# Row loads and final stores on one queue: a Trainium2 encoder step with the loads of the next group placed further back

## What is computed

```
h = rmsnorm(x, norm1_g)
z = h @ w_in                       # 1024 -> 1536 = [a | u | v], 512 columns each
u, v = gelu(u), gelu(v)
pool_out = trailing means of a over 2, 4, 8, 16 rows, minus a, per-group 128x128 map, scale
gmlp_out = u * (W_s v + b)         # in chunks of 128 rows, 4 heads, block-causal mask
x = x + concat(pool_out, gmlp_out) @ w_out
f = rmsnorm(x, norm2_g) @ w_up     # 1024 -> 4096
x = x + square(relu(f)) @ w_down   # 4096 -> 1024
y = rmsnorm(x, normf_g)
```

## Time and profile before

| what | us |
|---|---|
| median of 3 runs | 1239.54 |
| lowest and highest of the 3 | 1237.45, 1247.37 |
| the profiled execution, whole | 1246.71 |
| its span on the slowest core (core 1) | 1245.2 |
| its span on the fastest core (core 7) | 1212.4 |
| PE busy on core 1 | 1179.2 (95%) |
| DVE, ACT, POOL busy on core 1 | 803.9, 438.2, 156.8 |

### The profile page before, as it was taken

One profiled execution on the slowest core, in us unless ns is written; L12 is line 12 of the kernel. 1 busy time (PEld: TensorE's weight loads), 2 busy tenths in 40 slices (PEclk: granted clock), 3 DMA queues, 4 the chain that ended last, 5 costly groups with the idle time before them and its releaser, 6 DMA issues.

```text
span 1245.2 us, 21470 instructions; the slowest of 8 cores (1212.4 to 1245.2 us)
## 1 busy us (share of the span) xinstructions
PE 1179.2 (95%) x7412; PEld 701.2 (56%) x7412; DVE 803.9 (65%) x1164; ACT 438.2 (35%) x678; POOL 156.8 (13%) x303
## 2 busy tenths in 40 slices
PE   6889999988999999999999999997999999999996
PEld 2547456533444577446754577445764576547842
DVE  3564545386567675867587675865778575976773
ACT  3446022323410454134530364132640365233401
POOL 3111000113000220022100220021100220011001
PEclk7999999999899989999999999998999999999998
DMA  9996798989995895769767794769856896869993
GB/s 197 167 212 168 210 249 208 209 327 311 331 310 196 261 311 176 255 228 314 270 228 235 263 332 165 267 217 305 281 199 224 252 371 135 299 201 324 307 330 130
DMA packets 64907, 310.41 MB, mean 249 GB/s; under 512 B 9872, under 2 KB 9936, under 8 KB 44064
## 3 DMA queue, kind: packets, MB, share of 16 engines
q1 hardware_dynamic: 48992, 239.35, 57.9%
q0 software_dynamic: 15664, 69.15, 21.8%
q10 hardware_dynamic: 144, 0.52, 0.2%
HBM read 277.90 MB, written 53.31 MB: 266 GB/s over the span
## 4 chain that ended last, share of the span: by engine, by line
PE 73%; DMA 17%; DVE 3%; issue 3%; ACT 2%; POOL 1%; DVEq 0%; POOLq 0%; SPq 0%; ACTq 0%
PE ps L757 23%; PE ps L668 20%; PE ps L538 9%; PE ps L419 9%; DMA scr_up<-RING 5%; DMA yall<-XS 5%; PE ps L440 4%; PE ps L619 3%; PE ps L594 3%; DMA RING<-w_mlp 2%; DMA RING<-scr_up 2%; PE ps L373 2%; DMA XS<-xall 1%; ACT JUNK L350 1%; DMA scr_um<-RING 1%
## 5 line engine op out<-in xcount | busy, mean ns | idle before, releaser
L757 PE MATMUL ps<-RING,ST 128*128 128x512 bf16 x1120 | 256.9, 379 | 0.3 <-DVE ST L730 0.3
L350 ACT ACTIVATE JUNK<-XS 128x1024 bf16<-128x1024 f32 (+1 forms) x100 | 105.5, 1055 | 315.3 <-DVE XS L543 228.9
L668 PE MATMUL ps<-H2T,RING 128*128 128x256 bf16 x1536 | 184.1, 278 | 16.6 <-DVE ST L709 15.0
L757 PEld LDWEIGHTS ps<-RING,ST 128*128 128x128 bf16 x1120 | 108.7, 98 | 126.5 <-issue 1.7
L668 PEld LDWEIGHTS ps<-H2T,RING 128*128 128x128 bf16 x1536 | 152.2, 100 | 47.8 <-issue 20.1
L767 DVE TENSOR_TENSOR XS<-XS,ps 128x512 f32<-128x512 f32 x140 | 95.8, 685 | 75.3 <-PE ps L757 70.8
L668 PE MATMUL ps<-SB,RING 128*128 128x256 bf16 x1152 | 138.8, 273 | 3.9 <-DMA RING<-scr_um 2.2
L668 PEld LDWEIGHTS ps<-SB,RING 128*128 128x128 bf16 x1152 | 111.3, 98 | 20.4 <-issue 5.6
L719 ACT ACTIVATE ST<-ST 128x1024 bf16<-128x1024 bf16 x96 | 101.4, 1056 | 54.9 <-DVE ST L709 50.5
L419 PE MATMUL ps<-HT,WAU 128*128 128x512 bf16 (+2 forms) x512 | 118.0, 379 | 1.4 <-ACT HT L377 1.4
L709 DVE TENSOR_TENSOR ST<-PQ,ps 128x512 bf16<-128x512 f32 x96 | 61.7, 684 | 64.7 <-ACT PQ L705 37.5
(11 more groups left out here) (107 smaller groups left out, 1421.6 us busy)
## 6 DMA issues: line engine op xcount, KB each, us to landing
RING<-scr_dn SPq DMA_DIRECT2D x98, 1024.0 KB, 6.3
RING<-scr_um SPq DMA_DIRECT2D x120, 512.0 KB, 7.8
RING<-scr_up SPq DMA_DIRECT2D x48, 512.0 KB, 8.9
RING<-w_mlp POOLq DMA_DIRECT2D x16, 1024.0 KB, 14.8
yall<-XS POOLq DMA_DIRECT2D x29, 512.0 KB, 8.4
RING<-scr_wo SPq DMA_DIRECT2D x14, 1024.0 KB, 5.8
XS<-xall POOLq DMA_DIRECT2D x24, 512.0 KB, 7.9
scr_up<-RING POOLq DMA_DIRECT2D x8, 1024.0 KB, 14.1
```

What stands on the lines that cost most here:

```text
L350: add("act", lambda e: e.activation(out=JUNK[0:np_], in_=ap, func=AF.Square, scale=1.0 / 32, accum_out=SS[kind][0:np_, j:j + 1]), reads=re ...
L668: i_ = e.matmul(bank(ub)[:, u * 256:(u + 1) * 256], lhsT=RING[s][:, h * 4 + k, c0 + u * 128:c0 + (u + 1) * 128], rhs=op[:, k, :], start=(f ...
L757: i_ = e.matmul(bank(ub)[:, :], lhsT=lh(kk), rhs=RING[s][:, kk, :], start=(c == 0 and kk == 0 and M not in CONT), stop=(c == 1 and kk == 7 ...
```

## The change

The steps of five kinds of side work are renumbered. No operation is added or taken away.

- The loads of tiles 1 and 2 of group i + 2 leave down steps 22 and 25 of group i. They are recorded with the load of tile 3 in the up stage of the group after: tiles 1, 2 and 3 at up steps 1, 3 and 7 (`lx=(1, 3, 7)`), where tile 3 alone stood at step 6. At steps 1 and 7 a `final_out` of the same step is recorded ahead of the load. The load of tile 0 stays at down step 3.
- The four gates of a down stage stand one step earlier (4, 4, 6, 6), except for those of the plain group.
- In the plain group `N1_sq` of tile 2 stands at step 21 instead of 19. The new entry `us` is not used, and `lx` there names the step that the loads had.
- In both setup passes the fourth weight sum stands at step 11 instead of 12 and the fifth at 16 instead of 14, each with its `ring_done`.
- In pass 1 the four transposes `N2_T` of group 2 stand one step earlier (4, 5, 7, 8).

```diff
-                ws = dict(w=(5, 6, 10, 12, 14))
+                ws = dict(w=(5, 6, 10, 11, 16))
...
-                    for n in range(4):
-                        side(8, L(load_x, j, n))
...
+                    for n in range(4):
+                        side(tn["lx"][n], L(load_x, j, n))
...
                     if j < NG:
-                        side(tn["lx"], L(load_x, j, 3))
+                        for n in range(3):
+                            side(tn["lx"][n], L(load_x, j, n + 1))
...
                     if i + 2 < NG:
-                        side(d(dn["lx"][0]), L(load_x, i + 2, 0))
+                        side(d(dn["lx"]), L(load_x, i + 2, 0))
                     for n in range(2):
                         side(d(dn["fq"][n]), L(final_sq, i, n), L(final_rs, n, n + 1))
                         side(d(dn["fo"][n]), L(final_out, i, n))
-                        if i + 2 < NG:
-                            side(d(dn["lx"][1 + n]), L(load_x, i + 2, n + 1))
```

More of the change, by code:

```diff
@@ L960, in schedule @@
                 else:
-                    e1 = dict(v=(1, 3), pl=(0, 1, 2, 3), gt=(8, 8, 9, 10), wo=(14, 15, 16, 17, 18, 19, 20, 21), nq=(21, 22, 23, 24), rs=(23, 23, 25, 25), na=(2, 3, 4, 5), nt=(5, 6, 8, 9), fq=(16, 17, 18), fo=(19, 19, 19))
+                    e1 = dict(v=(1, 3), pl=(0, 1, 2, 3), gt=(8, 8, 9, 10), wo=(14, 15, 16, 17, 18, 19, 20, 21), nq=(21, 22, 23, 24), rs=(23, 23, 25, 25), na=(2, 3, 4, 5), nt=(4, 5, 7, 8), fq=(16, 17, 18), fo=(19, 19, 19))
                     for n in range(2):
@@ L1005, in schedule @@
                 if plain:
+                    tn = dict(sq=(15, 17, 21, 21), ap=(18, 20, 22, 24), tr=(23, 27, 27, 30), v=(36, 37, 39, 39), au=(31, 31, 33, 34, 35, 36, 37, 38), pl=(34, 36, 38, 39), us=(7, 7, 7, 7), lx=(8, 8, 8, 8))
                     side(0, *[L(final_sq, 1, n) for n in range(2)], L(final_rs, 0, 2))
@@ L1008, in schedule @@
                     for n in range(4):
-                        side(8, L(load_x, j, n))
-                    tn = dict(sq=(15, 17, 19, 21), ap=(18, 20, 22, 24), tr=(23, 27, 27, 30), v=(36, 37, 39, 39), au=(31, 31, 33, 34, 35, 36, 37, 38), pl=(34, 36, 38, 39))
+                        side(tn["lx"][n], L(load_x, j, n))
                 else:
-                    tn = dict(sq=(2, 5, 7, 11), ap=(3, 6, 9, 12), tr=(5, 8, 11, 14), v=(6, 11, 14, 19), au=(15, 16, 18, 18, 20, 21, 23, 24), pl=(18, 18, 21, 22), fq=(0, 0), fo=(1, 7), lx=6)
+                    tn = dict(sq=(2, 5, 7, 11), ap=(3, 6, 9, 12), tr=(5, 8, 11, 14), v=(6, 11, 14, 19), au=(15, 16, 18, 18, 20, 21, 23, 24), pl=(18, 18, 21, 22), fq=(0, 0), fo=(1, 7), lx=(1, 3, 7))
                     for n in (2, 3):
@@ L1016, in schedule @@
                     if j < NG:
-                        side(tn["lx"], L(load_x, j, 3))
+                        for n in range(3):
+                            side(tn["lx"][n], L(load_x, j, n + 1))
                 d = lambda k: d0 + k
-                dn = dict(s1=(0, 1, 2, 3), s7=(5, 5, 8, 9), s2=(10, 10, 11, 11), s6=(11, 11, 13, 12), sm=(12, 12, 13, 13), fq=(18, 20), fo=(21, 24), lx=(3, 22, 25), gt=(5, 5, 7, 7), wo=(10, 11, 12, 13, 14, 15, 16, 17), nq=(14, 15, 16, 17), na=(16, 16, 17, 18), nt=(17, 18, 19, 21), es=(25, 25, 26, 27, 27), u1=25)
+                dn = dict(s1=(0, 1, 2, 3), s7=(5, 5, 8, 9), s2=(10, 10, 11, 11), s6=(11, 11, 13, 12), sm=(12, 12, 13, 13), fq=(18, 20), fo=(21, 24), lx=3, gt=(4, 4, 6, 6), wo=(10, 11, 12, 13, 14, 15, 16, 17), nq=(14, 15, 16, 17), na=(16, 16, 17, 18), nt=(17, 18, 19, 21), es=(25, 25, 26, 27, 27), u1=25)
                 if plain:
```

## The result

Over 20 runs each the changed kernel took 1249.6 us (median), the kernel before 1241.3 us. The ratio is 1.0074, with a 95% interval of [1.0055, 1.0093]; measured again later beside new runs of the kernel before it was 1.0043 [1.0024, 1.0062]. So the change costs some 0.4 to 0.7%: small, inside the 1% that the prediction named as its limit, and real. The ratios leave out executions in which cores of one die ran at a lower granted clock.

What follows compares the result with a forecast made beforehand. PE, busy 95% of the span, was taken as the bound. Core 3: 1229.5 + 9.5 (late rows) + 1.7 (setup) = 1240.7; core 1: 1223.7 + 9.5 + 1.7 = 1234.9; forecast 1238 us between them, range 1226 to 1254.

Steps and rivals of the forecast that it cites:

- The chain store, load, store, load, root is cut: POOL's queue: two store-load pairs, some 12 us each on core 1, no longer stand ahead of a root PE needs.
- Its worth: 22.0 us on core 1: PE's L709 waits, 15.0 us, plus 7.0 us of lowered clock are saved on core 1; 1.9 us on core 3.
- The profiled execution stands 7.2 us above the median: The profiled execution is 7.2 us above the median of the runs shown; the median should lie between cores 3 and 1.
- The weights' loads give back 3.0 us: Up stage, core 3: half of PE's 6.0 us of weight waits is regained, between 0 and 6.0; about 1 on core 1.
- The load of tile 1 comes 3.9 us late for ACT: Up stage, behind the store of tile 2: rows land at 571.1, 3.9 us after ACT wants them at 567.25.
- That costs PE 1.9 us a boundary, 9.5 in all: After 2.0 us of slack, PE loses 1.9 us at each of five boundaries, 9.5 in all; range 0 to 30.
- Tiles 2 and 3 at nothing: Row loads of tiles 2 and 3 cost 0; if their cover fails, up to 1.9 us each, 19 in all.
- The setup: 1.7 us: Pass 1: PE reaches the wait for group 2's fourth `HB` one product earlier and loses 1.7 us on every core.
- The fastest core slower than 1212, the cores closer together: Sign that the forecast is right: core spans lie closer together, and the fastest is slower than 1212.
- clean: Rival: rows land in time and only the removal counts, about 1228 us; chance 0.25.
- Slower, by the clock: Rival: rows 5.7 us late, PE stands 3.7 us and the clock drops at each boundary, 1255 us; chance 0.15.
- The load still waits for a store: Rival: a moved row load still waits for a store, nothing won and the setup lost, about 1241 us; no-effect chance 0.10.

Runs made afterwards that it cites:

- The kernel with the loads behind the roots: Kernel before with row loads of tiles 1 and 2 at up step 0, behind both final roots, tile 3 at step 6: ratio 0.9911, again 0.9908.
- Loads behind the store: Kernel before with only the row loads moved as in the change (up steps 1, 3 and 7): ratio 1.0015 [0.9983, 1.0046].
- the copy: The changed kernel, unchanged, measured again beside the kernel before: ratio 1.0043 [1.0024, 1.0062], slowest core +4.9 us.

## Why the forecast was off

The forecast was no change, with 1238 against 1239.5 us. The truth is 5 to 9 us slower. What failed is the size of the removal; the late rows, which the prediction had found, cost about what it said. Step by step:

- *The chain store, load, store, load, root is cut, and PE's wait for L709 goes with it.* Right on every core. The chain itself was read rightly, though for the first of its loads name DVE's L658 as the releaser. The store of core 1 ahead of it shows that it was the landing: 837.61 + 11.2 = 848.8, and the load went at 849.71.

```profile
837.61 0.63 POOL L786 DMA_DIRECT2D yall<-XS  x1
...
DMA to landing us min/median/max: 11.2/11.2/11.2
```

- *Its worth: 22.0 us on core 1.* This is the step that failed. Without the setup's 1.7, the sum for a clean removal was 1246.7 - 1229.5 = 17.2 us on the slowest core. The kernel with the loads behind the roots is that clean removal, and it gains 7.9 and 10.8 us on the slowest core, 5.4 and 6.5 in the mean. So the term was too large by 6 to 9 us, which is most of the error. The 15.0 us of the earlier trace rows were read on the core that fared worst in one execution; the mean of the eight in that same profile was 5.9. With some 2 us for the clock, and 2.4 us more of waits for the ring loads in their place, that mean gives 5.5, about what was gained. The wait is a collision that falls on other cores each time, and with it gone on the slowest core the next slowest is not far. I did take core 3 as the one that comes last then, but gave it the waits of that one execution too.
- *The profiled execution stands 7.2 us above the median.* It did, above the median of those 3 runs, and it is high in their series as well, where comparable runs of the kernel before took 1233.6 to 1247.4 us. In the three later series 1246.7 was an ordinary time. A sum that takes away the waits of one execution should be compared with that execution: 1238 on 1246.7 is a forecast of 8.7 us faster. Setting it beside 1239.5 hid part of the overestimate and moved the wording to "no change".
- *The weights' loads give back 3.0 us.* Not shown, and in the clean removal it went the other way. PE's waits for `scr_um` and `scr_up` together are 4.1 and 4.3 us in the mean of the cores in the two profiles of before. They are 1.5 and 4.3 in those of the changed kernel, so the gain of 2.5 in the first pair is not there in the second. With the loads behind the roots they are 6.5. Core 1 there:

```profile
PE ps L668 <- DMA RING<-scr_up: 8.4, 8, 2.8
PE ps L668 <- DMA RING<-scr_um: 4.7, 8, 0.9
```

- *The load of tile 1 comes 3.9 us late for ACT.* Right in kind. It is right to a tenth on core 5 by luck: the load went 5.38 us after L697 as worked out, but landed in 10.5 us instead of 9.7 + 1.3 = 11.0, and ACT wanted it 12.1 us after L697 instead of the 12.5 of core 7. The mean of the 40 boundaries is 4.6.
- *That costs PE 1.9 us a boundary, 9.5 in all.* Close on a mild boundary (1.81), by a road that I had half seen: only 0.75 of it comes through L679 and L681, and 1.06 through the root, `HB` and the transposes. Too low in all. In the mean of the cores PE's waits for `HB` and L681 are 7.9 + 5.3 us against 0.9 before, 12.3 more. Loads behind the store against loads behind the roots is 750.4 - 738.0 = 12.4 us in the first-to-last measure, and 7.1 + 5.4 = 12.5 in the mean of the cores in one series. On the slowest core it is 2.8 + 7.9 = 10.7. So the term was mis-sized by 1 to 3 us. What lacked are boundaries at which the rows come later still, such as core 2's last, up to 7.3 us with the clock.
- *Tiles 2 and 3 at nothing.* Tile 2 yes. Tile 3 makes ACT wait 3 us, and costs some 0.6 us of PE's waits (2.2 at most) in all: nearly right.
- *The setup: 1.7 us; the fourth `HB` waits 5.5 us instead of 3.75 on core 1.* The size is about right (2 to 4 us in the mean in three series of executions, 0.6 in the two pairs of profiles up to the first L697). In the mean of the cores the wait grew by 1.7 us in the first pair and 2.9 in the second. On core 1 itself it was 7.62:

```profile
244.51 1.89 PE L594 MATMUL ps<-RING,ST 128*128 128x512 bf16 x8
254.02 1.01 PE L373 MATMUL ps<-IDB,HB 128*128 128x128 bf16 x8 [7.62 <-DVE HB L364]
```

DVE shows why: the sum in front of L364 waited 9.08 us for its float32 load and began at 250.28, 1.4 us later than before (248.89), while PE was there 2.5 us earlier.

```profile
250.28 2.29 DVE L608 TENSOR_TENSOR SB<-RING 128x4096 bf16<-128x4096 bf16 x1 [9.08 <-DMA RING<-w_mlp]
252.49 1.28 DVE L364 SCALAR_TENSOR_TENSOR HB<-XS,RS,G2B 128x1024 bf16<-128x1024 f32 x1
```

- *The fastest core slower than 1212, the cores closer together.* Right: 1227.7 to 1242.1.

Put together with measured sizes, for the slowest core: -8 to -11 for the removal, +11 for the late rows, +1 to +4 for the setup and the gates, which is +1 to +7 (the terms come from several series). The 4.9 us of the copy lies inside; the first measurement, 0.74% or 9 us, lies somewhat above, and that difference stays open.

Of the rivals, *clean* is wrong for this change and right for the version with the loads 3 us earlier, whose loads land at 572.0 and 575.7 against squares at 573.74 and later. *Slower, by the clock* happens at 10 of the 40 boundaries and not at all of them. *The load still waits for a store* is wrong: POOL's L404 has no wait for `yall` on any core.

The rule in the Trainium skill ("DMA: Bandwidth & Descriptors", section "Anatomy of one DMA — SWDGE (gpsimd) path") would have made the rows punctual, by an estimate of 3.2 us. The trace does not agree after the change either: 10.5 us.

## What to carry to other kernels

On an in-order queue price a load by what stands behind it and by the time it needs to land in the stage where it will run, and put it behind the small urgent work (here the roots) but ahead of a store that waits for another engine: in this kernel that order was worth 0.9%, and the one behind the store cost 7 us in the mean of the cores. Where eight cores run and the slowest counts, a wait that strikes one core per execution is better sized by the mean over cores than by the core that it struck in the one profile. And compare variants by the mean of the cores too: it told 7 us apart where the ratio of the slowest cores could not.

## What the hardware showed beyond that

- A second transfer on POOL's queue lands much later than its issue says. The store of core 5 issued at 565.17 took this long:

```profile
DMA to landing us min/median/max: 7.4/7.4/7.4
```

It landed at 572.6, the load issued 0.63 us behind it at 576.3: 3.7 us apart. The two loads of the other version, 0.6 us apart, landed at 572.0 and 575.7, 3.7 apart too. In the earlier trace rows, before the first L697 of the up stage, it was 1.3.
- A short wait of PE may cost only itself. On core 5 it stood 1.06 and 0.75 us, and the clock stayed full:

```profile
574.00:582.00 8.00, 6.19 (x57) 4.95 (x56) 3.93 (x5) 5.51 (x9) 0.79 (x2) 1.00 1.00 313
```

On core 2, after 3.11 and 0.75, the same 16 matmuls took 3.57 us instead of 1.91, at the level of 1.2 GHz. The sum of the two waits does not settle it. On core 5, two boundaries on, 1.62 and 0.76 were enough (row below), while 1.85 and 0.76 at the first boundary of core 2 left the 16 matmuls at 1.91.

```profile
860.77 3.54 PE L668 MATMUL ps<-SB,RING 128*128 128x256 bf16 x16 [0.76 <-DVE PQ L681]
```

- The wait for the float32 load in the setup differs widely from run to run. PE's wait for the fourth `HB` was 3.75 us on core 1 in the earlier trace rows and 7.62 there after the change; in the copy of the changed kernel it was 11.1 on core 5.
